# Eight sample tokens' delta-rule step: four rounds of three block-sum jobs become three joint read-out jobs and four outer-product jobs

## The reference, cut to what matters

```
sa = einsum('bhvk,bhk->bhv', S, -kk)
S  = S * w[:, :, None, :] + sa[..., None] * (kk * a)[:, :, None, :] + v[..., None] * k[:, :, None, :]
y  = einsum('bhvk,bhk->bhv', S, r)
```

## Time and profile before

| what | us |
|---|---|
| median of 3 runs | 808.62 (808.17 to 808.8) |
| the profiled execution's own time | 808.59 |
| its span, first to last instruction | 807.0 |
| PE busy / DVE busy / ACT busy | 778.5 / 432.6 / 211.1 |
| mean granted PE clock | 0.987 of full |

### The profile page before, as it was taken

The page is one execution under the profiler, slowest core; times in us unless marked ns, Lnnn a source line. Parts: engine busy times, 40 slices in busy tenths (PEclk is TensorE's granted clock), DMA queues, the critical chain, the costliest instruction groups (busy, mean ns, idle before and its releaser), DMA issues.

```text
span 807.0 us, 19996 instructions
## 1 busy us (share of the span) xinstructions
PE 778.5 (96%) x8538; PEld 536.5 (66%) x8538; DVE 432.6 (54%) x855; ACT 211.1 (26%) x497; POOL 39.6 (5%) x50
## 2 busy tenths in 40 slices
PE   7999999999999999999999999999999879999995
PEld 5877777787767877777777777767778643333331
DVE  4965667588777655566676555446313441011145
ACT  4222222254523312212212332220003411111134
POOL 0000000000000000000000000000000021222211
PEclk9999999999999999999999999999999979999998
DMA  9541432431212101111140012046735579999966
GB/s 328 184 160 52 128 110 70 180 106 57 97 55 80 54 28 56 51 33 42 47 158 29 29 54 82 3 168 263 305 149 210 210 297 422 386 390 386 394 230 220
DMA packets 36678, 127.19 MB, mean 158 GB/s; under 512 B 5827, under 2 KB 16099, under 8 KB 31728
## 3 DMA queue, kind: packets, MB, share of 16 engines
q1 hardware_dynamic: 32560, 115.78, 38.3%
q0 software_dynamic: 4032, 10.15, 4.3%
HBM read 106.83 MB, written 18.68 MB: 156 GB/s over the span
## 4 chain that ended last, share of the span: by engine, by line
PE 88%; DMA 4%; DVE 4%; ACT 2%; issue 1%; POOL 0%; SPq 0%; POOLq 0%; DVEq 0%; ACTq 0%
PE psum L1370 23%; PE psum L1351 12%; PE psum L1703 10%; PE psum L2616 9%; PE psum L1328 4%; PE psum L2650 3%; DMA arena<-u_rows,ids 2%; DVE arena L2050 2%; PE psum L1315 2%; PE psum L1303 2%; PE psum L1571 2%; PE psum L1659 1%; PE psum L1584 1%; PE psum L2596 1%; PE psum L1468 1%
## 5 line engine op out<-in xcount | busy, mean ns | idle before, releaser
L2050 DVE TENSOR_TENSOR arena<-arena 128x268 f32<-128x268 f32 (+10 forms) x322 | 175.3, 544 | 48.3 <-ACT arena L1802 28.9
L1370 PE MATMUL psum<-arena 128*128 128x268 f32 x784 | 189.5, 393 | 0.0
L1370 PEld LDWEIGHTS psum<-arena 128*128 128x128 f32 x784 | 145.1, 189 | 37.8 <-issue 11.6
L1802 ACT ACTIVATE arena<-psum 128x268 f32<-128x268 f32 (+7 forms) x215 | 85.7, 406 | 276.7 <-PE psum L1370 146.5
L2050 DVE TENSOR_TENSOR arena<-psum,arena 128x256 f32<-128x256 f32 (+5 forms) x170 | 71.7, 426 | 80.3 <-PE psum L1584 21.9
L1351 PE MATMUL psum<-arena 128*128 128x268 f32 x392 | 105.0, 402 | 0.0
L1703 PE MATMUL psum<-arena 128*128 128x268 f32 x384 | 91.0, 391 | 1.6 <-DVE arena L2050 1.2
L2616 PE MATMUL psum<-arena 128*32 128x512 f32 (+1 forms) x640 | 86.1, 600 | 0.5 <-DVE arena L2773 0.3
L1351 PEld LDWEIGHTS psum<-arena 128*128 128x128 f32 x392 | 69.7, 189 | 20.4 <-issue 6.3
L1703 PEld LDWEIGHTS psum<-arena 128*128 128x128 f32 x384 | 71.1, 189 | 17.7 <-issue 3.3
L2773 DVE TENSOR_TENSOR arena<-psum,arena 128x256 f32<-128x256 f32 (+2 forms) x38 | 24.3, 663 | 100.9 <-ACT arena L2685 84.6
(11 more groups left out here) (210 smaller groups left out, 695.8 us busy)
## 6 DMA issues: line engine op xcount, KB each, us to landing
arena<-in_w_gu SPq DMA_DIRECT2D x16, 2048.0 KB, 20.5
arena<-in_w_in SPq DMA_DIRECT2D x45, 512.0 KB, 4.3
arena<-in_w_dn SPq DMA_DIRECT2D x16, 1024.0 KB, 17.9
arena<-in_w_out SPq DMA_DIRECT2D x2, 2048.0 KB, 14.1
arena<-arena SPq DMA_DIRECT2D x5, 536.0 KB, 6.0
arena<-in_x SPq DMA_DIRECT2D x8, 268.0 KB, 5.9
arena<-arena SPq DMA_DIRECT2D x16, 134.0 KB, 4.5
arena<-in_x SPq DMA_DIRECT2D x1, 2144.0 KB, 14.5
```

The source lines that it names most:

```text
L1370: last = mm(ps, w[:, k, :], x[:, k, :], start=(k == 0 and i in (0, 1, 3)), stop=(k == KD // 2 - 1), skip_group_check=i not in (0, 1, 3))
L1802: run(nc.scalar.activation(out, in_, fn, **kw), s)
L2050: run(v.tensor_tensor(out, a, b, op), s)
```

## The change

All four head pairs are done together. `sm_a` 0 lays kk and r times w of each head into `smp_x` (zero elsewhere), and `j_sx` multiplies the old state by it: four matmuls, one per p, each 32 weight columns wide, 512 columns moving, into the four 32-partition strips of one bank. DVE keeps the own sequence's block (`own`) and reduces to `smp_r` (`sm_b`). `j_sr` turns that back to channels (two 64-wide matmuls of 128 columns) and adds the dot products b.r and k.r (one of 64 columns). `sm_y` makes -sa and y from them with five small operations. `j_st` transposes sa, v, b and k (eight matmuls, 32 wide, 128 columns); DVE spreads sa and v to 128 x 512 twice (`spread`) and keeps the keys. `j_so` p forms both outer products at once: two matmuls (one per head) with 16 contraction rows, 64 wide, 512 columns moving, and DVE adds the bank to ws (which `sm_w` p has decayed). When `j_so` 0 or 2 is taken, the next one is put right behind it. `j_mean` 0 to 3 are no longer side steps: they stand in a row at the end of the stretch of fill in chunk 5. A constant of 64 columns becomes one of 8. SP waits for the readers of `j_so` ahead of the `wkvs` output.

```diff
@@ take
             elif whole_job() and side and side[0][0].startswith("j_") and now[0] - made[0] >= 2:
                 out.append(side.pop(0))
+                if out[-1] in (("j_so", 0), ("j_so", 2)):
+                    out.append(side.pop(0))
@@ order
-    for p in range(NP):
-        side += [("sm_a", p, i) for i in range(3)] + [("j_sk", p), ("sm_b", p), ("j_sv", p), ("sm_c", p), ("sm_y", p),
-                                                      ("j_sy", p), ("sm_d", p)]
+    side += [("sm_a", 0), ("j_sx", 0), ("sm_a", 1), ("sm_b",), ("sm_a", 2), ("j_sr", 0), ("sm_w", 0), ("sm_y", 0), ("sm_y", 1), ("j_st", 0)]
+    side += [("sm_w", p) for p in range(1, NP)] + [("j_so", p) for p in range(NP)]
...
-        if c == 5:
-            side += [("j_mean", n) for n in range(NP)]
...
             while not whole_job():
                 s += take(1)
-            assert all(k == "j_mean" for k, _ in side), side
-            s += side
+            assert not side, side
+            s += [("j_mean", n) for n in range(NP)]
             side[:] = norms(0)
@@ PE
-                elif kind in ("j_sk", "j_sv", "j_sy"):
...
-                    mm(job_ps(step, 512), bones, (t2 if kind == "j_sv" else t1), start=True, stop=True)\
-                        .then_inc(s_job, 1)
+                elif kind == "j_sx":
+                    open_job(step)
+                    pe.wait_ge(s_smt, 1)
+                    for p in range(NP):
+                        last = mm(job_ps(step, 512)[32 * p:32 * p + 32], smp_x[:, p].rearrange("k s i b -> k (s i b)"),
+                                  ws[:, p].rearrange("k b v -> k (b v)"), start=True, stop=True)
+                    last.then_inc(s_job, 1)
+                elif kind == "j_sr":
+                    ps = open_job(step)
+                    pe.wait_ge(s_smt, 3)
+                    for s in range(2):
+                        mm(ps[64 * s:64 * s + 64, 0:P], smp_r, ident, start=True, stop=True)
+                    mm(ps[:, P:P + 2 * NP * NB], bones, smp_br.rearrange("k a p b -> k (a p b)"), start=True,
+                       stop=True).then_inc(s_job, 1)
+                elif kind == "j_st":
+                    ps = open_job(step)
+                    pe.wait_ge(s_smt, 4)
+                    for a in range(2):
+                        for p in range(NP):
+                            last = mm(ps[32 * p:32 * p + 32, P * a:P * a + P],
+                                      smp_z[:, p, 2 * a:2 * a + 4].rearrange("k i b -> k (i b)"), ident, start=True, stop=True)
+                    last.then_inc(s_job, 1)
+                elif kind == "j_so":
+                    p = step[1]
+                    open_job(step)
+                    job_read(pe, ("j_st", 0))
+                    r = slice(32 * p, 32 * p + 2 * NB)
+                    for s in range(2):
+                        last = mm(job_ps(step, 512)[64 * s:64 * s + 64], keys_t[r, 64 * s:64 * s + 64],
+                                  spread[r, s].rearrange("k b v -> k (b v)"), start=True, stop=True)
+                    last.then_inc(s_job, 1)
@@ DVE
+                elif kind == "sm_a":
+                    if step[1] == 0:
...
+                        run(v.memset(smp_x, 0.0))
+                        for s in range(2):
+                            h = slice(64 * s, 64 * s + 64)
+                            run(v.tensor_copy(smp_x[h, :, s, 0], kk_f[h, :, TP:T]))
+                            tt(smp_x[h, :, s, 1], r_f[h, :, TP:T], wsmp[h], s=s_smt if s else None)
+                    elif step[1] == 1:
+                        tt(smp_br[:, 0], smp(b_f), smp(r_f))
+                        tt(smp_br[:, 1], smp(k_f), smp(r_f), s=s_smt)
+                    else:
+                        for i, a in ((0, b_f), (1, k_f), (3, v_f), (4, b_f), (5, k_f)):
+                            run(v.tensor_copy(smp_z[:, :, i], smp(a)))
+                elif kind == "j_sx":
+                    job_done(dve, step)
+                    tt(smp_p, job_ps(step, 512).rearrange("k (b v) -> k b v", b=NB), bc(cc("own"), 64), s=free)
+                elif kind == "sm_b":
...
+                    run(v.tensor_reduce(smp_r, smp_p.rearrange("k b v -> k v b"), AX.X, ALU.add), s_smt)
...
+                elif kind == "j_st":
+                    job_done(dve, step)
+                    run(v.tensor_copy(keys_t, job_ps(step, P)))
+                    for s in range(2):
+                        x = bank(bank_of(step))[:, P + 64 * s:P + 64 * s + 64]
+                        tt(spread[:, s], x.unsqueeze(1).broadcast_to([P, NB, 64]), bc(cc("own"), 64), s=free if s else None)
+                elif kind == "j_so":
+                    p = step[1]
+                    job_done(dve, step)
+                    tt(ws[:, p], ws[:, p], job_ps(step, 512).rearrange("k (b v) -> k b v", b=NB), ALU.add, s=free)
```

More of the change, by code:

```diff
@@ L78 @@
 for _name, _w in [("ident", P), ("bones", P), ("ones", P), ("tri", P), ("reset", TP), ("lev", len(LEVELS) * H),
-                  ("lev0", 2 * H), ("eyeh", H), ("eye", C), ("ai", 2 * C), ("tie", 16),
+                  ("lev0", 2 * H), ("eyeh", H), ("own", NB), ("ai", 2 * C), ("tie", 16),
                   ("valid", TT), ("slot", SLOTS), ("more", ROUNDS - 1), ("split", 4 * TT),
@@ L124, in constants @@
     put("eyeh", rowh[:, None] == colh[None])
-    put("eye", row[:, None] == col[None])
+    put("own", p[:, None] % NB == np.arange(NB)[None])
     strict, incl = row[:, None] < col[None], row[:, None] <= col[None]
@@ L536, in hybrid_step @@
         smp0 = top[0]
-        t1 = at(512, NB, 64)
-        t2 = at(512, NB, 64)
+        top[0] += 1024
         wsmp = at(NP * NB, NP, NB)
+        smp_z = at(NP * 6 * NB, NP, 6, NB)
+        keys_t = at(P, start=smp0 + 1024 + NP * NB)
+        spread = at(1024, 2, NB, 64, start=smp0)
+        smp_p = at(512, NB, 64, start=smp0)
+        small0 = smp0 + 512
+        smp_x = at(4 * NP * NB, NP, 2, 2, NB, start=small0)
+        smp_r = at(64, start=small0 + 4 * NP * NB)
+        small0 += 4 * NP * NB + 64
+        smp_br, smp_o, smp_d, smp_t = [at(2 * NP * NB, 2, NP, NB, start=small0 + 2 * NP * NB * i) for i in range(4)]
         top[0] = max(top[0], raw0 + 4096 + 6144)
@@ L654, in hybrid_step @@
         s_ph = sem("s_ph")
-        s_ws = sem("s_ws")
         s_att = sem("s_att")
@@ L1210, in _ @@
             sp.dma_start(O["shift"], sh).then_inc(s_out, 16)
-            sp.wait_ge(s_ws, NP)
+            for p in range(NP):
+                job_read(sp, ("j_so", p))
             sp.dma_start(O["wkvs"], ws).then_inc(s_out, 16)
-            sp.wait_ge(s_ys, NP)
+            sp.wait_ge(s_ys, 1)
             for i in (SEVEN - 2, SEVEN - 1):
@@ new lines, in _ @@
+                elif kind == "sm_a":
+                    if step[1] == 0:
+                        dve.wait_ge(s_rets, 48)
+                        dve.wait_ge(s_sw, 1)
+                        run(v.memset(smp_x, 0.0))
[13 more added lines that the diff above has]
+                elif kind == "sm_b":
+                    job_read(dve, ("j_sx", 0))
+                    run(v.tensor_reduce(smp_r, smp_p.rearrange("k b v -> k v b"), AX.X, ALU.add), s_smt)
+                elif kind == "j_sr":
+                    job_done(dve, step)
+                    ps = bank(bank_of(step))
+                    for s in range(2):
+                        h = slice(64 * s, 64 * s + 64)
+                        run(v.tensor_copy(smp_o[h].rearrange("k i p b -> k p i b"),
+                                          ps[h, 0:P].rearrange("k (p s i b) -> k p s i b", p=NP, s=2, i=2)[:, :, s]))
+                    run(v.tensor_copy(smp_d, ps[:, P:P + 2 * NP * NB].rearrange("k (a p b) -> k a p b", a=2, p=NP)), free)
+                elif kind == "sm_y":
+                    if step[1] == 0:
+                        job_read(dve, ("j_sr", 0))
+                        ts(smp_z[:, :, 2], smp_o[:, 0], -1.0, None, ALU.mult, s=s_smt)
+                        tt(smp_t[:, 0], smp_z[:, :, 2], smp_d[:, 0])
+                        tt(smp_t[:, 1], smp(v_f), smp_d[:, 1])
+                    else:
+                        tt(smp_t[:, 0], smp_t[:, 0], smp_o[:, 1], ALU.add)
+                        tt(smp(ly), smp_t[:, 0], smp_t[:, 1], ALU.add, s=s_ys)
+                elif kind == "sm_w":
+                    p = step[1]
+                    tt(ws[:, p], ws[:, p], bc(wsmp[:, p, :], 64))
+                elif kind == "j_st":
+                    job_done(dve, step)
+                    run(v.tensor_copy(keys_t, job_ps(step, P)))
+                    for s in range(2):
+                        x = bank(bank_of(step))[:, P + 64 * s:P + 64 * s + 64]
+                        tt(spread[:, s], x.unsqueeze(1).broadcast_to([P, NB, 64]), bc(cc("own"), 64), s=free if s else None)
+                elif kind == "j_so":
+                    p = step[1]
+                    job_done(dve, step)
+                    tt(ws[:, p], ws[:, p], job_ps(step, 512).rearrange("k (b v) -> k b v", b=NB), ALU.add, s=free)
```

43 lines of the change are left out of this document (5 added, 38 removed).

## The result

The changed kernel takes 815.09 us (median of 4 runs, 814.2 to 816.14) where the kernel before, run beside it, took 808.39. The ratio is 1.0075, with a 95% interval of 1.0063 to 1.0088. I had forecast 807.7 and a range up to 811.0.

A forecast was written before the change was run, and what follows sets the result against it. PE was taken to bound the kernel (busy 778.5 of 807.0 us). 11.4 us out, less 6.1 of new PE work, 2.0 of pair waits and 2.4 of mean waits, gave 0.9 us less: 807.7, range 804.5 to 811.0.

The forecast's parts named there:

- What goes and what comes on PE: Block-sum jobs and five bank waits out, 11.4 us; narrow joint jobs and changes of tile in, 6.1 us.
- The first rival: The two halves of each `j_so` do not overlap: 1.72 us instead of 0.88, total 811.1; chance 0.14.
- The pairs: Both `j_so` of a pair share a bank; the second waits 1.02 us for DVE, 2.0 us for two pairs.
- the second rival: Waits in the pairs and the row of means are covered: 803.3, or 805.5 with half of them; chance 0.20.
- The means: Four `j_mean` in a row in one bank: three stand still 0.80 us each, 2.4 us.
- DVE's cover: DVE waits for PE before its recurrence steps, smallest idle 0.44 us, so DVE work was costed at nothing.
- third rival: A DVE or ACT recurrence step becomes late as PE work around it goes: 2.4 us, 810.1; chance 0.07.
- The sum: Whole kernel: 11.4 - 6.1 - 2.0 - 2.4 = 0.9 us less, 807.7.
- The range: Total time 804.5 to 811.0, said to reach from the second rival's half-covered case to the first rival.
- the half-covered case: Half of the waits in the pairs and the row of means are covered: 805.5.
- the forecast's own range: 806.2 to 809.2 for the total time, from the bounds of the waits; forecast's chance 0.52.
- The bound on `j_so`: Per outer-product job, forecast at 0.88 us: 0.44 if both jobs of a pair overlapped too, 1.72 if nothing overlaps.

The follow-up runs named there:

- e3: Changed kernel with the outer products (`j_so`) taken singly and the four means put back among the side steps as before; 805.63 us, ratio 0.9961.
- e1: Changed kernel with only the pairing undone: the four `j_so` jobs taken singly, each between the two parts of another fill job; 808.54 us, ratio 0.9993.
- e2: Changed kernel with the pairs left and the four mean jobs put back among the side steps as before; 811.87 us, ratio 1.0037.
- e8: e3 with `j_so` in pairs in one bank again, the second part of the open fill job between the members; 806.52 us, ratio 0.9984.
- e5: e3 with `j_so` in pairs again, each pair between two fill jobs so its members get different banks; 805.58 us, ratio 0.9965.
- e6: Kernel before with the block-sum job of v issued twice in one bank for head pairs 0 and 1, all rows active; 813.21 us, ratio 1.0054.
- e9: Changed kernel with its outer products over all 128 rows instead of 16, same pairs and waits; 810.52 us, ratio 1.0017.
- e10: e6 with the doubled job and the one before it as two 64-wide matmuls over 16 rows; 818.14 us, ratio 1.0103.
- e12: e3 with means 1 to 3 in a row ahead of part 113 and mean 0 ahead of part 101; 807.49 us, ratio 0.9988.
- e11: e3 run once more, unchanged, for its time against the kernel before; 805.96 us, ratio 0.9964.

## Why the prediction was wrong, point by point

- **What goes and what comes on PE**: forecast 11.4 - 6.1 = 5.3 us less. The changed kernel shows 4.6 us (above). Right, 0.7 too high. `j_sx` made the first chunk 1.23 us longer (27.07 for 25.84), where I had 0.98. The job and its change of tile take just 1.00 us, 289.60 to 290.60; the other 0.23 is the wait of the next fill job for its bank, of the kind that I took off five times on the side of what goes and never put on the side of what comes. The narrow groups overlap as the earlier trace rows said. So the trace's 0.11 us a record stands for `j_sx`, and not the 1.1 us a job that I estimated from the factor of 3.07 in the Trainium skill (TensorE: Matmul & The Clock Gate, packing small matmuls). The Trainium skill gives that factor for four tiles that split the rows; those of `j_sx` split the columns. The first rival (halves that don't overlap) is out: 1.0 us from one `j_so` to the fill behind it in e3 (348.59 to 349.60), not 1.8.
- **The pairs**: same bank, and from one member's start to the other's 1.94 us for the 0.88 + 1.02 forecast. Right, the second rival (covered waits) is out.
- **The means**: 2.3 us with the weights, for 2.4. Right.
- **DVE's cover** (third rival): no new wait of the recurrence's lines for DVE or ACT. Right. But the break in the L1549 group of chunk 5, 0.8 us, was in no term and no rival.
- **The sum**: by the forecast's own terms 4.6 - 2.0 - 2.3 = 0.3 us less than before, against 0.9. Measured is 6.3 more; the 6.6 between are 5.8 us of half clock and the 0.8 of the break. What failed is the price of the waits. I wrote that in the waits PE "has nothing" and priced them by their length. For the pairs their length is a third of their cost (2.0 of 6.5 us). I had read the clock of 1.00 in the earlier trace rows as a property of the stretch. It depends on what PE does there: 10.2 us at half clock behind the two pairs cost 4.7 us, and 3.4 us behind the means 1.1.
- **The range** ended at 811.0 for the first rival, not for the waits: their upper bounds (1.7 a pair, 3.7 for the means) were for DVE's queue and would give 810.4. Its lower end, 804.5, is what the waits' lower bounds give (0 and 1.2), not the half-covered case, which was 805.5; and the forecast's own range of 806.2 to 809.2 is narrower than these bounds.
- **The bound on `j_so`** took rows only as a question of overlap. That 16 rows instead of 128 take the same time but leave the clock less margin was in no rival.

By parts, the change is 3.7 us of gain (e3: 227.5 for 231.2 us; that is 4.6 less the 0.6 of its break in chunk 5, and an estimate of up to 0.4 for two more groups of outer products that stand alone, each with 0.1 into its tile shape and 0.1 back), the pairing costs 815.09 - 808.54 = 6.5 us (e1) and the row of means 815.09 - 811.87 = 3.2 (e2).

## What to carry to other kernels

Where PE is the bound, a new wait between two of its jobs has two prices: its length, and what follows if the granted clock goes down; read the clock in narrow windows behind each wait, and count waits that lie close together, and matmuls over few rows beside them, as one risk. Two jobs in a row that share a PSUM bank are such a wait; one part of unrelated work between them (e8, 806.5 us for 815.1) or a second bank (e5, 805.6) takes it away. When jobs are merged to save PE time, spend the saving on the same places as before: leave the reader's time behind each job.

## What the hardware did that I had not expected

- Two waits of 1.02 us, 6 us apart or more: granted clock 1.00 with matmuls over 128 rows on both sides (e6, e9), 0.5 for 6.8 us behind the first with 16 rows (changed, e10). Between the changed kernel and e9, columns, instruction counts and PE's time at full clock are the same.
- The clock came down behind the third of three waits of 0.70 us (472.7 us in the changed kernel) and did not behind two (e12), in the profiled executions.
- A stretch at half clock costs less than half its length: 4.7 us for 10.2 (changed against e9).
- A DVE reduction over a strided view of 128 x 512 took 1.03 us where the contiguous one took 0.69 (so does the plain operation in the earlier trace rows); it lies beside PE work.

```profile
L2366 DVE TENSOR_REDUCE arena<-arena 128x64 f32<-128x512 f32 x1 | 1.0, 1031 | 0.0
```

What stays open: how often the clock falls at these places, since each kernel has one profiled execution; how near to the edge pairs without a wait are (e8's two long executions); what breaks the L1549 group of chunk 5; and why the stretch at half clock near 645 us, present in every kernel, is longer in some executions (13.7 us with a tail of 303.0 us in the profiled execution of before and 303.1 in e3, 17.1 us with 304.4 in the changed one and 305.1 in e11).
